# First tile projected block by block, meta tokens second, row scaling moved behind the input projection

## The chip, the cores and the metric

The kernel runs on one core of one Trainium2 chip. The metric is the device time of one execution in microseconds (us). The kernel before took 2399.41 us, the median of three runs (2391.92, 2399.41 and 2402.00).

## The reference, cut to what matters

One encoder block over 1024 tokens of width 1024, with 16 learned meta tokens put in front. What the change touches is its first step, the normed input projection, and the order of the token tiles in it:

```python
h = jnp.concatenate([meta, x], axis=1)            # 16 + 1024 rows
a = rms_norm(h, attn_norm_g[l])                   # x * rsqrt(mean(x*x) + eps) * g
proj = a @ w_in[l]                                # 1024 -> 1184 columns
q_s, k_s, v_s, q_lat, kv_lat, k_rope = jnp.split(proj, split_at, axis=-1)
# widths 512, 128, 128, 256, 128, 32
q_s, k_s = rms_norm(per head of 64, both)         # windowed attention
q = rms_norm(q_lat, g) @ w_q_up; kv = rms_norm(kv_lat, g) @ w_kv_up
q, k = rms_norm per head, then rope on 32 of 96   # latent attention
...
h = h + jnp.concatenate([y_a, y_b], axis=-1) @ w_out[l]
h = h + moe_ffn(rms_norm(h, ffn_norm_g[l]), ...)
return h[:, N_META:]                              # meta rows are dropped
```

The meta tokens serve as keys and values only; their queries are not needed for the output. Row scaling by the root of the mean square commutes with the product by `w_in`, which is what lets it be done behind the projection.

## The kernel before, in words

The program has three stages with a barrier between them: `project` (this change), `attend` and `experts`. Each is written by hand as one instruction stream for each engine, with semaphores between them; there is no scheduler. Every engine works strictly in the order in which its stream is written.

`project` goes over nine tiles of rows: eight real tiles of 128 and, as the last (t = 8, `MT`), the 16 meta tokens. SyncE (SP) loads tile 0, then the eight 128-row blocks of `w_in`, then the other tiles into three buffers `xt`. For one tile:

- `x_stats` (ScalarE) sums the squares and takes the root; `x_norm` (VectorE, L349) takes the reciprocal and multiplies the whole 128x1024 tile by it.
- `transpose_x` (TensorE, L488) turns the scaled tile into two PSUM banks; `norm_copy` on ScalarE (first four blocks) and on VectorE (last four) copies them to `normT`.
- `proj_part` (TensorE, L478) makes the 1184 columns in three parts of 512, 160 and 512, each over eight blocks of `w_in`, each in its own bank; `proj_copy` (ScalarE, L256) copies each part to `proj`. In the trace every fp32 matmul is two records, so a part is 16.
- The chain behind it, called the post work here: VectorE squares and sums `proj`, ScalarE takes roots, VectorE scales the heads (`qn`) and latents (`lat`) and signals `lat_ready`; TensorE transposes them (jobs `qpairs`, `lats`), makes the up projections (`kv0`, `kv1`, `q0`, `q1`); VectorE norms and rotates the heads (`k_ready`, `q_ready`); TensorE transposes them (`kT0` to `qT1`); ScalarE copies every job out of three rotating banks.

The main loop runs in steps s from -1 to 8. In step s TensorE does, in this order, part 0 of tile s+1, the transposes behind `lat_ready` of tile s, part 1 of tile s+1, the up projections of tile s, part 2 of tile s+1, the transposes of tile s+2, and the head transposes of tile s. So the projection of the next tile lies in the waits of the post work of this one. On VectorE a step begins with `x_norm(s + 2)`, which waits for ScalarE's `x_stats(s + 2)`, and only then comes the post work. `w_in` is multiplied by the norm's gain on VectorE (L369), block by block; TensorE waits for all eight blocks before its first projection:

```python
if s == -1:
    pe.wait_ge(w_scaled, DC)
proj_part(s + 1, 0)
```

After `project`, `attend` starts with its own loads: its first VectorE work waits for the load of `sink`, issued at the start of the stage.

Of the kernel before, what the change touches and what calls it, by code (L numbers as in the profile page):

```python
# [20 lines left out]
ALU = mybir.AluOpType  # L21
# [87 lines left out]
def project(nc, io, keep):  # L109

    with ExitStack() as ctx:
# [54 lines left out]
        x_normed = m.sem("x_normed")  # L166
# [21 lines left out]

        jobs = []
        for t in range(MT + 1):  # L190
# [25 lines left out]
        with nc.Block() as block:  # L216

            @block.sync
            def _(sp):
                def load_x(t):  # L220
                    if t >= 3:
                        sp.wait_ge(xT_done, 2 * (t - 2))
                    src = io["meta_tokens"] if t == MT else io["x"][0, t * P:(t + 1) * P, :]
                    sp.dma_start(xt[0:rows(t), t % 3, :], src).then_inc(x_in[t % 3], 16)
# [4 lines left out]
                for t in range(1, MT + 1):  # L229
                    load_x(t)  # L230

            @block.gpsimd
            def _(pool):
                nc.gpsimd.memset(mla_g[:], 1.0).then_inc(gains_one, 1)
                for t in range(MT + 1):
                    n = rows(t)
                    pool.wait_ge(proj_out, 3 * t + 3)
                    nc.gpsimd.tensor_copy(swa_v[0:n, t, :], proj[0:n, t % 2, C_V:C_QL]).then_inc(v_copied, 1)

            @block.scalar  # L240
            def _(act):
# [6 lines left out]
                def x_stats(t):  # L248
                    n = rows(t)
                    act.wait_ge(x_in[t % 3], 16 * (t // 3 + 1))  # L250
                    link(nc.scalar.activation(square[0:n, :], xt[0:n, t % 3, :], ACT.Square,
                                              accum_out=x_stat[0:n, t, 0:1]))
                    nc.scalar.activation(x_stat[0:n, t, 1:2], x_stat[0:n, t, 0:1], ACT.Sqrt,
                                         scale=1.0 / D, bias=keep["eps"][0:n, :]).then_inc(x_root, 1)

                def proj_copy(t, part):  # L256
# [38 lines left out]
                def norm_copy(t):  # L295
                    if t >= 2:
                        act.wait_ge(proj_done, 3 * (t - 1))
                    act.wait_ge(xT_done, 2 * t + 1)
                    nc.scalar.copy(normT[:, t % 2, 0:4, 0:rows(t)],
# [1557 lines left out]
```

## Time and profile before

| | |
|---|---|
| median of three runs | 2399.41 us |
| the profiled execution, its own time | 2405.51 us |
| its span, first to last instruction | 2403.9 us |
| TensorE busy | 2267.3 us (94%) |
| VectorE, ScalarE, GpSimd busy | 779.9, 459.1, 216.2 us |
| stage `project`, from the start to the first matmul of `attend` | 256.76 us |
| mean granted TensorE clock | 0.971 |

All durations below are of the one profiled execution, which was 6.1 us above the median of the other runs. In the rows of a timeline the columns are the start and the duration in us, the engine, line and operation, what is written and read, the shapes, the count, and in brackets the idle time before it on this engine with what ended it. PE is TensorE, PEld its weight loads, DVE VectorE, ACT ScalarE. A row with a count merges neighbours.

### The profile page before, as it was taken

How to read it: one execution, taken by the hardware profiler on the slowest of the kernel's cores; microseconds unless marked ns; L12 is line 12 of the kernel's file. 1: busy time of each engine (PE TensorE's matmuls, PEld its weight loads, DVE VectorE, ACT ScalarE, POOL GpSimd, SP SyncE). 2: the span in 40 equal slices, each digit the busy share in tenths (PEclk: the TensorE clock that was granted, in tenths of full speed). 3: DMA queues.
4: the chain of work that ended last, by engine and by line, in shares of the span. 5: the costliest groups of instructions: out<-in, count | busy, mean ns of one | idle time of the engine just before them, and what ended most of it. 6: DMA issues, size and time to landing. Idle time of an engine off the chain costs nothing.

```text
span 2403.9 us, 36883 instructions
## 1 busy us (share of the span) xinstructions
PE 2267.3 (94%) x15236; PEld 1702.6 (71%) x15236; DVE 779.9 (32%) x2243; ACT 459.1 (19%) x1148; POOL 216.2 (9%) x248
## 2 busy tenths in 40 slices
PE   6999799999999639999999999999999999999997
PEld 3554466666666437788877887788788787887875
DVE  3555344454444412222222222222222222222221
ACT  2333334453444300000001000100000000100000
POOL 0000000000000110111111111111010000100000
PEclk9999799999999859999999999999999999999999
DMA  4000500000000196778887988799989989899881
GB/s 153 27 2 1 160 10 28 18 10 28 27 27 28 38 345 226 251 250 291 282 308 250 308 312 317 264 312 321 339 309 339 343 311 339 307 336 346 307 304 19
DMA packets 212010, 492.26 MB, mean 205 GB/s; under 512 B 24608, under 2 KB 28480, under 8 KB 211664
## 3 DMA queue, kind: packets, MB, share of 16 engines
q1 hardware_dynamic: 183888, 449.53, 51.2%
q0 software_dynamic: 16080, 38.27, 7.0%
q10 hardware_dynamic: 11872, 2.06, 0.5%
q8 instruction: 123, 2.02, 0.3%
q14 instruction: 47, 0.39, 0.0%
HBM read 464.59 MB, written 29.82 MB: 206 GB/s over the span
## 4 chain that ended last, share of the span: by engine, by line
PE 63%; ACTq 1%; DMA 1%; DVE 0%; issue 0%; POOL 0%; ACT 0%; POOLq 0%; DVEq 0%
PE gu_bank L1676 40%; PE ya_bank L1690 18%; PE yb_bank L1703 3%; PE xa_bank L1646 1%; ACTq L1489 1%; DMA tri_e<-in_tri 1%; PE xb_bank L1654 0%; ACTq L1487 0%; ACTq L1492 0%; POOL out_y L1425 0%; ACT y_rows L1503 0%; DVE y_rows L1561 0%; PE yb_bank L1713 0%; DVE xT L1577 0%; PE yb_bank L1711 0%
## 5 line engine op out<-in xcount | busy, mean ns | idle before, releaser
L1676 PEld LDWEIGHTS gu_bank<-xT,ring 128*128 128x128 f32 x8192 | 964.6, 191 | 15.7 <-issue 15.7
L1676 PE MATMUL gu_bank<-xT,ring 128*128 128x128 f32 (+10 forms) x8192 | 968.1, 281 | 1.0 <-DVE xT L1577 1.0
L1690 PE MATMUL ya_bank<-ring,hidden 128*128 128x512 f32 x1024 | 446.2, 594 | 0.0
L1690 PEld LDWEIGHTS ya_bank<-ring,hidden 128*128 128x128 f32 x1024 | 192.0, 190 | 230.0 <-issue 225.5
L1538 DVE TENSOR_SCALAR g_in<-gu_bank,bias_cur 128x128 f32<-128x128 f32 (+10 forms) x256 | 92.0, 359 | 683.7 <-PE gu_bank L1676 683.7
L1497 ACT ACTIVATE sig<-g_in 128x128 f32<-128x128 f32 (+10 forms) x256 | 81.0, 317 | 879.2 <-DVE g_in L1538 879.2
L1561 DVE TENSOR_TENSOR y_rows<-ya_bank,b_row 128x512 f32<-128x512 f32 x64 | 41.2, 686 | 383.1 <-PE ya_bank L1690 383.1
L484 PE MATMUL proj_bank<-w_in_sb,normT 128*128 128x512 f32 (+3 forms) x432 | 149.0, 499 | 13.5 <-DVE w_in_sb L369 12.7
L1425 POOL DMA_INDIRECT out_y<-y_rows,tab x32 | 51.9, 1620 | 960.9 <-ACT y_rows L1503 960.9
L1037 PE MATMUL score_bank<-mla_kT,mla_qT 96*128 96x512 f32 x256 | 137.2, 663 | 0.0
L1503 ACT ACTIVATE y_rows<-y_rows,tab 128x512 f32<-128x512 f32 x64 | 42.7, 714 | 478.2 <-DVE y_rows L1561 478.2
L484 PEld LDWEIGHTS proj_bank<-w_in_sb,normT 128*128 128x128 f32 (+1 forms) x432 | 70.6, 181 | 81.6 <-issue 78.2
L943 DVE TENSOR_REDUCE real_max<-score_bank 128x1 f32<-128x1024 f32 x64 | 78.4, 1225 | 118.1 <-PE score_bank L1037 117.9
L1158 PE MATMUL score_bank<-w_out_sb,mixedT 128*128 128x512 f32 x256 | 112.0, 595 | 1.6 <-issue 1.6
L792 ACT COPY probsT<-act_bank 128x512 f32<-128x512 f32 (+2 forms) x96 | 52.0, 542 | 245.4 <-PE act_bank L1060 199.6
L1158 PEld LDWEIGHTS score_bank<-w_out_sb,mixedT 128*128 128x128 f32 x256 | 48.0, 190 | 60.4 <-issue 60.4
L1541 DVE TENSOR_SCALAR u_in<-gu_bank,bias_cur 128x128 f32<-128x128 f32 (+10 forms) x256 | 89.7, 350 | 0.0
L551 POOL DMA_INDIRECT slot_table<-pair,slot_i x32 | 31.4, 981 | 543.7 <-DVE slot_i L912 535.7
L1550 DVE SCALAR_TENSOR_TENSOR hidden<-u_in,g_sig 128x128 f32<-128x128 f32 (+10 forms) x256 | 76.8, 300 | 8.8
L1037 PEld LDWEIGHTS score_bank<-mla_kT,mla_qT 96*128 96x128 f32 x256 | 47.7, 204 | 44.5 <-issue 44.5
L1547 DVE TENSOR_TENSOR g_sig<-g_in,sig 128x128 f32<-128x128 f32 (+10 forms) x256 | 74.4, 291 | 0.0
L1079 PE MATMUL mla_bank<-probsT,mla_v 128*64 128x128 f32 x1024 | 71.8, 284 | 0.0
(243 smaller groups left out, 1732.4 us busy)
## 6 DMA issues: line engine op xcount, KB each, us to landing
ring<-in_w_gate SPq DMA_DIRECT2D x64, 2048.0 KB, 12.9
ring<-in_w_up SPq DMA_DIRECT2D x64, 2048.0 KB, 10.9
ring<-in_w_down SPq DMA_DIRECT2D x64, 2048.0 KB, 14.0
b_row<-in_b_down SPq DMA_DIRECT2D x32, 512.0 KB, 9.9
w_in_sb<-in_w_in SPq DMA_DIRECT2D x8, 592.0 KB, 9.0
xt<-in_x SPq DMA_DIRECT2D x8, 512.0 KB, 4.0
resid<-in_x SPq DMA_DIRECT2D x8, 512.0 KB, 4.3
out_y<-resid SPq DMA_DIRECT2D x8, 512.0 KB, 2.6
```

What stands on the lines that cost most here:

```text
L484: last = nc.tensor.matmul(proj_bank[0:n, part, 0:c1 - c0], normT[:, t % 2, k, 0:n], w_in[:, k, c0:c1], start=(k == 0), stop=(k == DC - 1))
L943: link(v.tensor_reduce(real_max[:, n % 2:n % 2 + 1], score_bank[:, j % 2, :], AX.X, ALU.max))
L1037: last = nc.tensor.matmul(bank[:, half * 512:(half + 1) * 512], mla_qT[:, i, cols(t)], mla_kT[:, i, half * 512:(half + 1) * 512], start=Tr ...
L1158: last = nc.tensor.matmul(score_bank[:, j % 2, half * 512:(half + 1) * 512], mixedT[:, k, :], w_out[:, k, half * 512:(half + 1) * 512], st ...
L1497: nc.scalar.activation(sig[:, f % 2, 0:width], g_in[:, f % 2, 0:width], ACT.Sigmoid, scale=ALPHA)\
L1538: v.tensor_scalar(g_in[:, f % 2, 0:width], gu_bank[:, f % 2, 0:width], bias_cur[:, f:f + 1], LIMIT, ALU.add, ALU.min).then_inc(g_ready, 1)
L1541: v.tensor_scalar(u_in[:, f % 2, 0:width], gu_bank[:, f % 2, 256:256 + width], bias_cur[:, FC + f:FC + f + 1], 1.0 + LIMIT, ALU.add, ALU.min)\
L1547: v.tensor_tensor(g_sig[:, s % 2, 0:width], g_in[:, s % 2, 0:width], sig[:, s % 2, 0:width], ALU.mult).then_inc(g_sig_ready, 1)
L1550: v.scalar_tensor_tensor(hidden[:, s, 0:width], u_in[:, s % 2, 0:width], 1.0 - LIMIT, g_sig[:, s % 2, 0:width], ALU.max, ALU.mult).then_in ...
L1676: last = nc.tensor.matmul(gu_bank[:, f % 2, i * 256:i * 256 + width], w[:, k, c * P:(c + 1) * P], xT[:, k, 0:width], start=(k == 0), stop= ...
L1690: last = nc.tensor.matmul(ya_bank[:, h, :], hidden[:, k, 0:P], w[:, k % 4, h * 512:(h + 1) * 512], start=(k == 0), stop=(k == FC - 1))
L1703: last = nc.tensor.matmul(yb_bank[j * q:(j + 1) * q, 0:c], hidden[:, k, P:P + q], w[:, k % 4, j * c:(j + 1) * c], start=(k == 0), stop=(k ...
```

## The change

Four things are changed, all in `project`.

1. The tile is transposed as it was loaded. `x_norm` becomes `x_scale`, the reciprocal alone, and the scale is applied by ScalarE when it copies the projection out of PSUM (`proj_copy`).
2. The first tile is projected by `first_proj`: block k of `w_in` is used for all three parts as soon as that block has been multiplied by the gain. The transposes of the second tile stand ahead of it in TensorE's stream.
3. The order of the tiles is 0, meta, 1, ..., 7. What was counted by tiles is now counted by steps, through `order`.
4. Of the meta tile only 160 + 256 = 416 columns are projected (`meta_parts`): no windowed queries, no query latent.

ScalarE's stream has `norm_copy(0)` ahead of `x_stats(0)` and of the loads of the constants.

```diff
+        order = [0, MT] + list(range(1, MT))
+        LAST = len(order) - 1
+        meta_parts = [None, (C_KVL, C_END), (C_K, C_QL)]
...
             @block.sync
-                def load_x(t):
-                    if t >= 3:
-                        sp.wait_ge(xT_done, 2 * (t - 2))
+                def load_x(s):
+                    t = order[s]
+                    if s >= 3:
+                        sp.wait_ge(xT_done, 2 * (s - 2))
+                        sp.wait_ge(x_root, s - 2)
...
             @block.scalar
+                def proj_copy(s, part):
+                    t = order[s]
+                    if part_cols(t, part) is None:
+                        return
                     n = rows(t)
-                    c0, c1 = PROJ[part]
-                    if part == 0 and t >= 2:
-                        act.wait_ge(lat_ready, t - 1)
-                        act.wait_ge(v_copied, t - 1)
-                    act.wait_ge(proj_done, 3 * t + part + 1)
-                    nc.scalar.copy(proj[0:n, t % 2, c0:c1], proj_bank[0:n, part, 0:c1 - c0]).then_inc(proj_out, 1)
+                    c0, c1 = part_cols(t, part)
+                    if s >= 2:
+                        act.wait_ge(lat_ready, s - 1)
+                        act.wait_ge(v_copied, s - 1)
+                    act.wait_ge(x_scaled, s + 1)
+                    act.wait_ge(proj_done, parts_to(t, part))
+                    nc.scalar.activation(proj[0:n, s % 2, c0:c1], proj_bank[0:n, part, 0:c1 - c0], ACT.Copy,
+                                         scale=x_stat[0:n, s, 2:3]).then_inc(proj_out, 1)
...
+                norm_copy(0)
                 x_stats(0)
...
-                norm_copy(0)
                 x_stats(1)
+                norm_copy(1)
...
             @block.vector
-                def x_norm(t):
-                    n = rows(t)
-                    dve.wait_ge(x_root, t + 1)
-                    link(v.reciprocal(x_stat[0:n, t, 2:3], x_stat[0:n, t, 1:2]))
-                    v.tensor_scalar(xt[0:n, t % 3, :], xt[0:n, t % 3, :], x_stat[0:n, t, 2:3], None,
-                                    ALU.mult).then_inc(x_normed, 1)
+                def x_scale(s):
+                    n = rows(order[s])
+                    dve.wait_ge(x_root, s + 1)
+                    v.reciprocal(x_stat[0:n, s, 2:3], x_stat[0:n, s, 1:2]).then_inc(x_scaled, 1)
...
-                x_norm(0)
-
+                norm_copy(0)
                 dve.wait_ge(g_attn_in, 16)
                 for k in range(DC):
...
-                    if k == 1:
-                        norm_copy(0)
+                    if k == 3:
+                        x_scale(0)
...
+                    if t < MT:
+                        link(v.tensor_tensor(proj_sq[0:n, :], pr, pr, ALU.mult))
...
+                    else:
+                        v.tensor_tensor(proj_sq[0:n, C_K:C_V], pr[:, C_K:C_V], pr[:, C_K:C_V], ALU.mult)
+                        link(v.tensor_tensor(proj_sq[0:n, C_KVL:C_END], pr[:, C_KVL:C_END], pr[:, C_KVL:C_END], ALU.mult))
...
             @block.tensor
+                def first_proj():
+                    for k in range(DC):
+                        pe.wait_ge(w_scaled, k + 1)
+                        for part, (c0, c1) in enumerate(PROJ):
+                            last = nc.tensor.matmul(proj_bank[:, part, 0:c1 - c0], normT[:, 0, k, :],
+                                                    w_in[:, k, c0:c1], start=(k == 0), stop=(k == DC - 1))
+                            if k == DC - 1:
+                                last.then_inc(proj_done, 1)
+
+                def transpose_x(s):
+                    n = rows(order[s])
+                    pe.wait_ge(x_in[s % 3], 16 * (s // 3 + 1))
...
                         if s == -1:
-                            pe.wait_ge(w_scaled, DC)
-                        proj_part(s + 1, 0)
+                            transpose_x(1)
+                            first_proj()
+                        else:
+                            proj_part(s + 1, 0)
```

The first place is the start of TensorE's stream. `xT_bank<-ident_sb,xt` are the transposes of a loaded tile, `proj_bank` the projection, `job_bank` the post work. Before:

```order
L496 MATMUL xT_bank<-ident_sb,xt 128x128 x8
L484 MATMUL proj_bank<-w_in_sb,normT 128x512 x8
L484 MATMUL proj_bank<-w_in_sb,normT 128x160 x8
L484 MATMUL proj_bank<-w_in_sb,normT 128x512 x8
L496 MATMUL xT_bank<-ident_sb,xt 128x128 x8
L484 MATMUL proj_bank<-w_in_sb,normT 128x512 x8
L475 MATMUL job_bank<-ident_sb,qn 128x128 x4
```

And now:

```order
L550 MATMUL xT_bank<-ident_sb,xt 128x128 x8
L550 MATMUL xT_bank<-ident_sb,xt 128x16 x8
L537 MATMUL proj_bank<-w_in_sb,normT 128x512
L537 MATMUL proj_bank<-w_in_sb,normT 128x160
L537 MATMUL proj_bank<-w_in_sb,normT 128x512 x2
...
L517 MATMUL job_bank<-ident_sb,qn 128x128 x4
L517 MATMUL job_bank<-ident_sb,lat 128x128 x4
L529 MATMUL proj_bank<-w_in_sb,normT 16x160 x8
L581 MATMUL job_bank<-w_kvup,latT 128x512 x2
L586 MATMUL job_bank<-w_qup,latT 128x384 x4
L529 MATMUL proj_bank<-w_in_sb,normT 16x256 x8
```

The transposes of the second tile (meta, 16 wide) moved ahead of the first projection, and between the first projection and the first transposes of the post work no projection stands any more, where eight matmuls of 512 columns stood.

The second place is the end of TensorE's stream in `project`, the last two steps (`k_raw` and `q_raw` are the heads to be transposed). Before:

```order
L475 MATMUL job_bank<-ident_sb,qn 128x128 x4
L475 MATMUL job_bank<-ident_sb,lat 128x128 x4
L484 MATMUL proj_bank<-w_in_sb,normT 16x160 x8
L524 MATMUL job_bank<-w_kvup,latT 128x512 x2
L529 MATMUL job_bank<-w_qup,latT 128x384 x4
L484 MATMUL proj_bank<-w_in_sb,normT 16x512 x8
L475 MATMUL job_bank<-ident_sb,k_raw 96x128 x8
L475 MATMUL job_bank<-ident_sb,q_raw 96x128 x8
L475 MATMUL job_bank<-ident_sb,lat 128x16 x2
L524 MATMUL job_bank<-w_kvup,latT 16x512 x2
L475 MATMUL job_bank<-ident_sb,k_raw 96x16 x8
```

And now:

```order
L529 MATMUL proj_bank<-w_in_sb,normT 128x512 x8
L517 MATMUL job_bank<-ident_sb,k_raw 96x128 x8
L517 MATMUL job_bank<-ident_sb,q_raw 96x128 x8
L517 MATMUL job_bank<-ident_sb,qn 128x128 x4
L517 MATMUL job_bank<-ident_sb,lat 128x128 x4
L581 MATMUL job_bank<-w_kvup,latT 128x512 x2
L586 MATMUL job_bank<-w_qup,latT 128x384 x4
L517 MATMUL job_bank<-ident_sb,k_raw 96x128 x8
L517 MATMUL job_bank<-ident_sb,q_raw 96x128 x8
```

The stage now ends with the whole post work of a real tile, with queries, where it ended with the short one of the meta tile.

The third place is the start of ScalarE's stream, now (before, `normT` stood behind the loads of the constants):

```order
L275 DMA ident_sb<-in_ident 128x128
L276 DMA g_attn<-in_attn_norm_g 128x8x1
L336 ACT_TABLE_LOAD
L336 COPY normT<-xT_bank 128x512
L282 ACTIVATE square,x_stat<-xt 128x1024
L284 ACT_TABLE_LOAD
L284 ACTIVATE x_stat<-x_stat,eps 128x1
L344 DMA g_ql<-in_mla_q_lat_norm_g 128x2x1
```

The copy of the first tile moved ahead of the constants' fifteen loads, which thereby moved behind it.

## Rows read from the trace of the kernel before

**Rows 1.** Timeline of the first 51 us: start, duration, instruction, idle before.

```profile
9.65 1.94 PE L496 MATMUL xT_bank<-ident_sb,xt 128*128 128x128 f32 x8 [9.65 <-DVE xt L353]
...
17.46 1.58 DVE L369 TENSOR_SCALAR w_in_sb<-w_in_sb,g_attn 128x1184 f32<-128x1184 f32 x2 [7.96 <-DMA g_attn<-in_attn_norm_g]
...
24.27 17.66 PE L484 MATMUL proj_bank<-w_in_sb,normT 128*128 128x512 f32 x48 [12.67 <-DVE w_in_sb L369]
...
41.96 0.59 ACT L263 COPY proj<-proj_bank 128x512 f32<-128x512 f32 x1 [6.57 <-PE proj_bank L484]
...
44.44 0.16 DVE L352 RECIPROCAL x_stat<-x_stat 128x1 f32<-128x1 f32 x1 [0.91 <-ACT x_stat L253]
...
45.31 1.38 DVE L408 TENSOR_TENSOR proj_sq<-proj 128x1184 f32<-128x1184 f32 x1
...
50.64 0.66 PE L475 MATMUL job_bank<-ident_sb,qn 128*128 128x128 f32 x4
```

**Rows 2.** DMA issues from 5.9 us, and at 142.8 us: size, us to landing.

```profile
w_in_sb<-in_w_in SPq DMA_DIRECT2D x1, 592.0 KB, 12.4
xt<-in_x SPq DMA_DIRECT2D x1, 512.0 KB, 13.7
...
xt<-in_meta_tokens SPq DMA_DIRECT2D x1, 64.0 KB, 2.0
```

**Rows 3.** Timeline of TensorE's weight loads in the first projection.

```profile
25.26 0.33 PEld L484 LDWEIGHTS proj_bank<-w_in_sb,normT 128*128 128x128 f32 x1 [0.52 <-issue]
26.11 0.33 PEld L484 LDWEIGHTS proj_bank<-w_in_sb,normT 128*128 128x128 f32 x1 [0.52 <-issue]
```

**Rows 4.** Timeline of one step in the middle, 195 to 218 us.

```profile
196.53 1.04 ACT L251 ACTIVATE square<-xt 16x1024 bf16<-16x1024 f32 x1
...
198.20 0.74 DVE L353 TENSOR_SCALAR xt<-xt,x_stat 16x1024 f32<-16x1024 f32 x1
198.87 1.37 DVE L408 TENSOR_TENSOR proj_sq<-proj 128x1184 f32<-128x1184 f32 x1
...
204.19 0.66 PE L475 MATMUL job_bank<-ident_sb,qn 128*128 128x128 f32 x4 [1.63 <-DVE lat L429]
...
204.89 0.69 ACT L271 ACTIVATE swa_qT<-job_bank,swa_g 128x512 f32<-128x512 f32 x1 [1.63 <-PE job_bank L475]
...
207.30 1.88 PE L524 MATMUL job_bank<-w_kvup,latT 128*128 128x512 f32 x4
...
209.02 2.74 PE L529 MATMUL job_bank<-w_qup,latT 128*128 128x384 f32 x8
...
217.52 0.42 DVE L457 TENSOR_TENSOR q_raw<-proj_sq,head_root 128x256 f32<-128x256 f32 x1
```

**Rows 5.** Timeline of TensorE: starts of steps 1 and 7, then the stage's end.

```profile
67.53 4.89 PE L484 MATMUL proj_bank<-w_in_sb,normT 128*128 128x512 f32 x11
...
221.04 7.04 PE L484 MATMUL proj_bank<-w_in_sb,normT 128*16 128x512 f32 x16
...
229.03 2.35 PE L484 MATMUL proj_bank<-w_in_sb,normT 128*16 128x160 f32 x16
...
243.69 1.04 PE L475 MATMUL job_bank<-ident_sb,q_raw 128*96 128x128 f32 x8
...
247.81 0.29 PE L475 MATMUL job_bank<-ident_sb,lat 16*128 16x16 f32 x2 [3.08 <-DVE lat L429]
...
248.44 2.89 PE L524 MATMUL job_bank<-w_kvup,latT 128*16 128x512 f32 x4 [0.34 <-ACT latT L277]
...
256.76 3.57 PE L1026 MATMUL swa_bank<-mla_kT,mla_qT 96*128 96x16 f32 x16 [0.55 <-PEq L216]
```

**Rows 6.** Windows of the stage's end: busy times, PEclk (granted clock), DMA share, GB/s.

```profile
249.00:250.00 1.00, 1.00 (x3) 0.15 (x1) 0.00 (x0) 0.34 (x2) 0.00 (x0) 0.59 0.00 0
...
266.00:268.00 2.00, 0.86 (x2) 0.00 (x0) 0.00 (x0) 0.00 (x0) 0.00 (x0) 0.94 0.39 158
```

**Rows 7.** Timeline of `attend`: the first instruction of VectorE.

```profile
271.01 0.29 DVE L880 COPY meta_s<-swa_bank 128x128 f32<-128x128 f32 x1 [15.68 <-DMA sink<-in_swa_sink]
```

More of the change, by code:

```diff
@@ L185, in project, with part_cols, parts_to, parts_free @@
         pool_own = m.sem("pool_own_p")
+        order = [0, MT] + list(range(1, MT))
+        step_of = {t: s for s, t in enumerate(order)}
+        LAST = len(order) - 1
+        meta_parts = [None, (C_KVL, C_END), (C_K, C_QL)]
+        def part_cols(t, part):
+            return (meta_parts if t == MT else PROJ)[part]
+        def parts_to(t, part):
+            done = 0
+            for u in order:
+                for p in range(3):
+                    done += part_cols(u, p) is not None
+                    if (u, p) == (t, part):
+                        return done
+        def parts_free(t, part):
+            for u in reversed(order[:step_of[t]]):
+                if part_cols(u, part) is not None:
+                    return parts_to(u, part)
+            return 0
+        def tiles_to(s):
+            return sum(t < MT for t in order[:s])
         jobs = []
-        for t in range(MT + 1):
+        for t in order:
             names = ("qpairs", "lats", "kv0", "kv1", "q0", "q1", "kT0", "kT1", "qT0", "qT1")
@@ L228, in _ @@
                     sp.dma_start(w_in[:, k, :], io["w_in"][0, k * P:(k + 1) * P, :]).then_inc(w_in_in[k], 16)
-                for t in range(1, MT + 1):
-                    load_x(t)
+                for s in range(1, LAST + 1):
+                    load_x(s)
             @block.gpsimd
@@ L234, in _ @@
                 nc.gpsimd.memset(mla_g[:], 1.0).then_inc(gains_one, 1)
-                for t in range(MT + 1):
+                for s, t in enumerate(order):
                     n = rows(t)
-                    pool.wait_ge(proj_out, 3 * t + 3)
-                    nc.gpsimd.tensor_copy(swa_v[0:n, t, :], proj[0:n, t % 2, C_V:C_QL]).then_inc(v_copied, 1)
+                    pool.wait_ge(proj_out, parts_to(t, 2))
+                    nc.gpsimd.tensor_copy(swa_v[0:n, t, :], proj[0:n, s % 2, C_V:C_QL]).then_inc(v_copied, 1)
             @block.scalar
@@ L293, in job, with norm_copy @@
                     last.then_inc(job_out, 1)
[L295 to L299, printed above, removed]
-                                   xT_bank[:, 0, :].rearrange("p (k q) -> p k q", q=P)[:, :, 0:rows(t)])\
+                def norm_copy(s):
+                    n = rows(order[s])
+                    if s >= 2:
+                        act.wait_ge(proj_done, parts_to(order[s - 2], 2))
+                    act.wait_ge(xT_done, 2 * s + 1)
+                    nc.scalar.copy(normT[:, s % 2, 0:4, 0:n],
+                                   xT_bank[:, 0, :].rearrange("p (k q) -> p k q", q=P)[:, :, 0:n])\
                         .then_inc(normT_lo, 1)
+                norm_copy(0)
                 x_stats(0)
@@ L309, in _ @@
                         act.dma_start(dst, src).then_inc(const_in, 16)
-                norm_copy(0)
                 x_stats(1)
-                for s in range(-1, MT + 1):
+                norm_copy(1)
+                for s in range(-1, LAST + 1):
                     if s >= 0:
-                        n = rows(s)
-                        if s + 2 <= MT:
+                        t, n = order[s], rows(order[s])
+                        if s + 2 <= LAST:
                             x_stats(s + 2)
@@ L501, in _ @@
                 transpose_x(0)
-                for s in range(-1, MT + 1):
-                    n = rows(max(s, 0))
-                    if s + 1 <= MT:
+                for s in range(-1, LAST + 1):
+                    t = order[max(s, 0)]
+                    n = rows(t)
+                    if s + 1 <= LAST:
                         pe.wait_ge(normT_lo, s + 2)
```

148 lines of the change are left out of this document (75 added, 73 removed).

## The prediction, as put on record before the run

> **What bounds the kernel now.** I read the timeline of the first 51 us first, then one step in the middle, then the end of the stage, then the windows for the clock. All edits lie in `project`, the first 256.76 us [rows 5]; behind it `attend` starts by itself: its first VectorE work waits for its own load of `sink`, 14.3 us after the first matmul of the stage (271.01 - 256.76) [rows 7, 5]. So what `project` ends earlier or later should pass to the end one to one, and nothing more.
>
> Within `project` TensorE is the bound, with three exceptions. (a) The start: it stands idle until 24.27, when VectorE has scaled the last block of `w_in`; VectorE could begin at 17.46 only, when the gain's load had landed [rows 1]. (b) 1.63 us in each middle step, in which TensorE waits for `lat_ready` [rows 4]. (c) The end: from 244.73 (243.69 + 1.04) to 256.76, 12.03 us, only the meta tile's post work is left [rows 5]. Between these, step 0 ends at 67.53, the six steps 1 to 6 take 25.6 us each (221.04 - 67.53, over 6), step 7 takes 23.7 (to 244.73) [rows 5].
>
> I build the new stage from those pieces, as a sum of times along TensorE.
>
> **Start.** Transposing without the scaling takes the first transposes from 9.65 to about 6, which buys nothing, since the weights are not there. The first block is scaled at 17.46 + 0.79 = 18.3 [rows 1]; nothing in the change moves the gain's load. But TensorE's stream now has the transposes of the meta tile ahead of `first_proj`, and the meta tile's load is issued by SP behind all eight blocks of `w_in`. The last block landed 12.4 us after an issue at about 5.4, at 17.8, and the tile behind it 13.7 us after 5.95, at 19.7 [rows 2]. The 64 KB of meta rows took 2.0 us alone [rows 2], and in the queue I put them an eighth of a tile's 1.9 us behind the last block: 18.1. So the words "as the weights land" hold only in part: all the weights have landed when TensorE starts. Eight 16-wide transposes, about 1.1 us on a slow clock, give a start at 19.3, bounded by 18.3 (no wait for meta) and 21.0 (meta lands as late as a whole tile did). Of the expected start I take 5.0 us gained.
>
> The Trainium skill ("DMA: Bandwidth & Descriptors", Queues, rings and completion order) says that each DMA engine consumes the descriptors of one ring in order, which speaks against the block-by-block start, as here; it also says that loads are not finished strictly in that order. By the first the start is 19.3, by the second it could be 18.3. The two rows of landings above are in order.
>
> `first_proj` is the same 48 passes in another order, so again 17.66 us [rows 1], 1.6 of them the price of the half clock: weight loads 0.85 us apart at the start [rows 3] where 16 passes take 7.04 later, 0.43 each [rows 5]. VectorE needs 0.79 us for a block and TensorE 2.0 or more, so it does not starve. End: 37.0.
>
> ScalarE's part-2 copy with a scale takes 0.69 instead of 0.59, read from its copy of `swa_qT` with the scale of a partition [rows 4, 1]; the other copies are as long but lie in waits. Then come `x_stats` and VectorE's reciprocal (44.44 - 41.96 = 2.48 before, with a `norm_copy` of 0.5 in it that is gone): squares start at 39.2, and `lat_ready` comes 5.3 us later (50.64 - 45.31) [rows 1], at 44.6. The constants' loads are issued some 2 us later on ScalarE, because `norm_copy(0)` and a later `x_stats(0)` stand ahead; VectorE's work on them should then end near 34, before 37: no cost, and 3 us of room.
>
> **Step 0 loses its cover.** Before, part 0 of the next tile filled the wait for `lat_ready`. Now TensorE is idle from 37.0 to 44.6, 7.6 us. It was slow after the idle time before 24.27 [rows 1, 3], and at the stage's end the granted clock fell to half (1.2 GHz) at about 249.4, 4.7 us after the last dense work [rows 6, 5]; so I expect the half clock at 44.6. Full clock came back after 3.3 us (1.6 us lost at half speed) the first time, and only at about 266.1, 9.4 us after work resumed at 256.76, the second [rows 1, 3, 5, 6]. At full clock the step would take: from `qn`'s transposes to the kv matmuls 3.1 (207.30 - 204.19; the meta part of 160 columns costs the same 2.35 as a real one), from there to `q_ready` 10.6 (217.94 - 207.30) [rows 4, 5], and about 1.0 for the eight q transposes: 14.7. VectorE sets this length; the 256 columns of the meta part (half of 7.04) fit inside. With the half clock for 3.3 us it is 16.8, for 9.4 us 19.9; I take a return after 5 us, 17.7. Step 0 ends at 62.3, before 67.53: 5.2 gained.
>
> **Meta step.** Post work of the meta tile beside the projection of tile 1. It is like step 7 before (23.7), without the q up projections (2.6), `qn`'s transposes (0.5), q head transposes (0.9), with narrower k transposes (0.4) and `lat` (0.3), and with a tile to transpose (0.9): 19.9. Its shorter VectorE chain is done when TensorE's part 0 ends, so there is no wait.
>
> **Middle steps.** Five with `x_scale` (s = 2 to 6), then s = 7. The 128x1024 multiply of 0.74 stood on the path to `lat_ready`: ScalarE's squares at 196.53, multiply at 198.20, squares of `proj` at 198.87, TensorE's wait of 1.63 [rows 4]. It goes, with 0.7 us a step, and a wait of 0.9 remains: 24.9 each, 124.5; I take 124.1, as the first follows a step without q copies. Step 7 is the old 23.7 (no `x_norm` there either) with transposes of a tile neither before nor now, the projection 128 wide instead of 16, which costs the same; less the small difference of banks, 23.3. Sum so far 62.3 + 19.9 + 124.1 + 23.3 = 229.6, where before step 7 ended at 244.73: 15.1 gained.
>
> **End.** Now a whole post work is bare. From the end of the q transposes: `lat_ready` 4.0 later (part 2 ended 2.1 earlier; copy and squares start 0.8 after that, then 5.3), 2.0 to the kv matmuls with no projection between, 10.6 to `q_ready` [rows 4], 1.9 for the last transposes and ScalarE's copies, 0.3 for the barrier: 18.9 against 12.03. TensorE idles 4 us, works 1.3, and later idles 9, so by the fall seen after 4.7 us of idle and light work [rows 5, 6] part of this runs at half clock: 0.4 at least (final transposes), 6.3 if all do (1.2 for the first transposes, 1.7 for kv, 2.6 for q, 0.8 for the last). I take 3.6: 22.5. `attend` starts at 252.1 instead of 256.8.
>
> **Sum.** Start -5.0; step 0 -0.2 more; meta step and middle steps against the old steps 1 to 7 -9.9 (167.3 for 177.2); end +10.5; in all -4.6. The profiled execution's 2405.5 would become 2400.9; it lies 6.1 above the median, so the prediction for the median is 2399.4 - 4.6 = 2395.
>
> **Rivals.**
> *The clock stays up.* Idle of 3.08 us at 247.81 left the clock full for a while [rows 5, 6], so both new gaps might cost little: step 0 14.7 and end 19.3, 6.2 less: 10.8 gained, 2388.6. Against it: the 12.67 us gap was followed by the half clock [rows 1, 3], and 7.6 is nearer to that than to 3.
> *The lost cover costs more than the start brings (slower).* If half clock holds through all of step 0, kv starts 7.2 after `lat_ready`, kv and q work is 4.3 longer, the last transposes 1 longer: 24.3, and 1.7 more is lost in the meta step's first matmuls, 8.3 above my figure; with the end all at half clock, 2.7 more. Then +6.4: 2405.8. It decides from a return of the clock later than 9.4 us after 44.6, the longest seen [rows 5, 6]. Against it: this work is busier than that at 256.76, for TensorE has no long wait in it.
> The Trainium skill ("TensorE: Matmul & The Clock Gate", HAM oscillation) holds that bursts of matmuls with waits between them can fall to the slow clock at each wait; by that both gaps are paid, which my sum does in part, and without it 2388.6 would stand. The trace agrees at 249.4.
> *The early start doesn't come.* Meta rows land with a whole tile's delay, start at 21.0: 1.7 less gained, 2396.5. *The wait (b) was not the multiply's.* If ScalarE's longer copies (0.1 each) or its order delay `x_stats` as much as the multiply took, 3.5 less: 2398.3.
>
> **How the numbers follow.** Forecast 0.60, clock stays up 0.14, slower rival 0.08, late start 0.08, no gain in (b) 0.05; 0.05 for something behind `project` that my reading leaves out. What this kernel's runs can tell from no change is about 0.5%, 12 us. The forecast and most rivals are within it. Faster by more needs the full clock and an early start, or the runs' own scatter of some 5 us on top: 0.16. Slower by more needs the slower rival and scatter: 0.06. Same 0.78. Range: from the clock rival with 18.3 and scatter, 2384, to near the slower rival, 2404.
>
> **What would show it.** Right: the first projection starts near 19.3, behind 16-wide transposes that waited for the meta load; TensorE waits about 7.6 us for `lat_ready` of tile 0, with PEclk 0.5 behind it; middle steps of 24.9 with waits of 0.9; the last q copies about 22 us after the last projection's step; `attend`'s first matmul near 252; everything behind shifted alone. Wrong: a start at 24 or later, steps of 25.6, the constants' work ending later than 37, or a difference that arises behind the first matmul of `attend`.

## The result and the profile after

The changed kernel took 2406.38 us (median of 8 runs, 2402.95 to 2409.61), the kernel before 2398.61 us (8 runs, 2391.92 to 2402.0): ratio 1.0036, 95% interval 1.0022 to 1.0049. So it is 0.36% slower, 7.8 us by the medians, where 4.6 us faster was forecast. The profiled execution took 2409.1 us (before 2405.51), its span is 2407.1 us (before 2403.9), 3.2 us more.

In the edited stage the forecast held in its parts, with 2.7 us gained where 4.6 were forecast; the loss arose 580 us behind it. Timeline of TensorE in the kernel after, in `project` (columns as in the timelines above):

```profile
19.62 1.00 PE L550 MATMUL xT_bank<-ident_sb,xt 16*128 16x16 f32 x8 [11.80 <-DMA xt<-in_meta_tokens]
20.55 19.23 PE L537 MATMUL proj_bank<-w_in_sb,normT 128*128 128x512 f32 x48
...
47.45 1.09 PE L517 MATMUL job_bank<-ident_sb,qn 128*128 128x128 f32 x4 [7.67 <-DVE lat L471]
...
64.04 7.03 PE L529 MATMUL proj_bank<-w_in_sb,normT 128*128 128x512 f32 x16
...
84.33 7.11 PE L529 MATMUL proj_bank<-w_in_sb,normT 128*128 128x512 f32 x16 [0.42 <-ACT normT L336]
...
116.03 0.66 PE L517 MATMUL job_bank<-ident_sb,qn 128*128 128x128 f32 x4 [0.89 <-DVE lat L471]
...
207.37 7.03 PE L529 MATMUL proj_bank<-w_in_sb,normT 128*128 128x512 f32 x16
...
229.33 1.26 PE L517 MATMUL job_bank<-ident_sb,q_raw 128*96 128x128 f32 x8
234.79 1.00 PE L517 MATMUL job_bank<-ident_sb,qn 128*128 128x128 f32 x4 [4.20 <-DVE lat L471]
...
237.38 3.78 PE L581 MATMUL job_bank<-w_kvup,latT 128*128 128x512 f32 x4 [0.74 <-ACT latT L313]
...
254.09 3.57 PE L1083 MATMUL swa_bank<-mla_kT,mla_qT 96*128 96x16 f32 x16 [1.03 <-PEq L245]
```

They are read against [rows 1, 4, 5]: the first projection waits for the meta tile's load, the wait for `lat_ready` in the middle steps is 0.89 for 1.63, the uncovered wait of step 0 is 7.67, and the stage ends with a bare post work, part of it at half clock (kv in 3.78 for 1.88). `attend` begins at 254.09, before 256.76: 2.7 us gained. On VectorE, in the same window, the last blocks of `w_in`:

```profile
20.99 3.06 DVE L405 TENSOR_SCALAR w_in_sb<-w_in_sb,g_attn 128x1184 f32<-128x1184 f32 x4
```

VectorE was done with the eighth block at 24.05. TensorE's 48 passes, begun at 20.55, stand in one row without a wait. So the waits for single blocks held nothing up, and they, in place of one wait for all eight, are what let the projection start 3.5 us before the last block was scaled.

| piece, us | before | forecast | after |
|---|---|---|---|
| first projection starts | 24.27 | 19.3 | 20.55 |
| it takes | 17.66 | 17.7 | 19.23 |
| `lat_ready` of tile 0, as TensorE goes on | 50.64 | 44.6 | 47.45 |
| step 0 from there to the next step | 16.9 | 17.7 | 16.6 |
| step 1 (before tile 1, now the meta tile) | 25.6 | 19.9 | 20.3 |
| steps 2 to 6 | 127.9 | 124.1 | 123.0 |
| step 7 | 23.7 | 23.3 | 23.2 |
| its end to `attend` | 12.0 | 22.5 | 23.5 |
| `attend` begins | 256.76 | 252.1 | 254.09 |
| `attend`, to ScalarE's first load of `experts` | 579.4 | 579.4 | 577.9 |
| from there to the first gate matmul | 49.6 | 49.6 | 58.2 |
| from there to the end | 1518.1 | 1518.1 | 1517.0 |

The span's 3.2 us are -2.7 - 1.5 + 8.6 - 1.1 (rounded). What TensorE waits for at the start of `experts` is the plan of the expert blocks on VectorE, which needs ScalarE's small loads; `tri_e` is the last of them. ScalarE's loads and VectorE's first plan instruction, before:

```profile
836.15 0.61 ACTq L1487 DMA_DIRECT2D biasT<-in_b_gate  x1
836.80 2.42 ACTq L1487 DMA_DIRECT2D biasT<-in_b_up  x1
839.26 20.39 ACTq L1489 DMA_DIRECT2D masks<-in_masks  x1
...
861.96 0.53 ACTq L1492 DMA_DIRECT2D tri_e<-in_tri  x1
...
877.64 0.18 DVE L1582 TENSOR_TENSOR picked_e<-placing,widths 32x32 f32<-32x32 f32 x1 [4.32 <-DMA tri_e<-in_tri]
```

And after:

```profile
831.97 0.61 ACTq L1544 DMA_DIRECT2D biasT<-in_b_gate  x1
832.61 4.80 ACTq L1544 DMA_DIRECT2D biasT<-in_b_up  x1
...
837.45 29.56 ACTq L1546 DMA_DIRECT2D masks<-in_masks  x1
...
869.38 1.52 ACTq L1549 DMA_DIRECT2D tri_e<-in_tri  x1
...
882.01 0.18 DVE L1639 TENSOR_TENSOR picked_e<-placing,widths 32x32 f32<-32x32 f32 x1 [2.42 <-DMA tri_e<-in_tri]
```

ScalarE is held in the issue of `masks` for 29.56 us instead of 20.39. The loads are the same; no line of this stage was changed. The difference begins with the first of them. DMA views of both from the start of the stage (size, us from issue to landing), before and then after:

```profile
biasT<-in_b_gate ACTq DMA_DIRECT2D x1, 128.0 KB, 7.1
biasT<-in_b_up ACTq DMA_DIRECT2D x1, 128.0 KB, 36.2
```

```profile
biasT<-in_b_gate ACTq DMA_DIRECT2D x1, 128.0 KB, 14.8
biasT<-in_b_up ACTq DMA_DIRECT2D x1, 128.0 KB, 46.7
```

The first bias load lands 7.7 us later after its issue. At the same time SyncE begins its 2 MB weight loads. Before, its first was issued 1.41 us behind ScalarE's first load, after, 0.98 us. SyncE's own instructions (view by source line, SyncE's address arithmetic and first load), before:

```profile
L1327 SPq FUSED_REGOPS  x1: 48/48/48, 837.0 to 837.0; - x1
L1327 SPq MOVE ring<-in_w_gate x1: 29/29/29, 837.5 to 837.5; - x1
L1327 SPq DMA_DIRECT2D ring<-in_w_gate x1: 426/426/426, 837.6 to 837.6; - x1
```

And after:

```profile
L1384 SPq FUSED_REGOPS  x1: 48/48/48, 832.8 to 832.8; - x1
L1384 SPq MOVE ring<-in_w_gate x1: 38/38/38, 832.9 to 832.9; - x1
L1384 SPq DMA_DIRECT2D ring<-in_w_gate x1: 420/420/420, 832.9 to 832.9; - x1
```

(Columns: count, ns min/median/max, first and last start.) Before, SyncE stood 0.4 us between two instructions (837.0 to 837.5, the first 48 ns long); after, it does not stand there. It stands elsewhere. SyncE's last load of `attend` and its first instruction of the barrier, before:

```profile
L765 SPq DMA_DIRECT2D ffn_rows<-normed_r x1: 319/319/319, 823.5 to 823.5; - x1
L734 SPq DRAIN  x1: 123/123/123, 823.9 to 823.9; - x1
```

And after:

```profile
L822 SPq DMA_DIRECT2D ffn_rows<-normed_r x1: 320/320/320, 819.3 to 819.3; - x1
L791 SPq DRAIN  x1: 107/107/107, 820.1 to 820.1; - x1
```

The load ends at 823.8 and the next instruction follows at 823.9 in the first; it ends at 819.6 and the next follows at 820.1 in the second. So the pause is now ahead of the barrier, where SyncE waits 12 us for the other engines anyway, and it costs nothing there. Counted through the traces of all 13 kernels, a pause of 0.44 to 0.45 us stands ahead of the 80th recorded instruction of SyncE in every one of them, six recorded waits more or fewer. The theory that was tested by the runs below: this pause belongs to a place in SyncE's instruction stream; the six added waits in `load_x` move it out of the start of `experts`, SyncE comes 0.43 us earlier against ScalarE, and ScalarE's small loads meet the weights before the first is done. The rival: the loss belongs to the edits of `project` or varies by itself.

The six waits stand in the change's diff, but among its four points they are not named. The tile is transposed as it was loaded, so its transposes no longer show that ScalarE has summed its squares, and a load into its buffer has to wait for both.

### The profile page after: what moved, and what is told of

The parts are those of the page before. It is cut to its first block, busy times and chain, and to the rows that moved or that the text cites. A ratio compares the mean times of both kernels' runs of the same rounds, so it can differ in the third digit from the quotient of the medians.

```text
span 2407.1 us, 36887 instructions
## 1 busy us (share of the span) xinstructions
PE 2262.8 (94%) x15220; PEld 1705.3 (71%) x15220; DVE 771.5 (32%) x2234; ACT 460.8 (19%) x1147; POOL 216.0 (9%) x248
## 4 chain that ended last, share of the span: by engine, by line
PE 63%; ACTq 2%; DMA 1%; DVE 0%; issue 0%; POOL 0%; ACT 0%; POOLq 0%; DVEq 0%
PE gu_bank L1733 40%; PE ya_bank L1747 18%; PE yb_bank L1760 3%; ACTq L1546 1%; PE xa_bank L1703 1%; DMA tri_e<-in_tri 1%; PE xb_bank L1711 0%; ACTq L1544 0%; ACTq L1549 0%; POOL out_y L1482 0%; ACT y_rows L1560 0%; DVE y_rows L1618 0%; PE yb_bank L1770 0%; DVE xT L1634 0%; PE yb_bank L1768 0%
## 5 line engine op out<-in xcount | busy, mean ns | idle before, releaser
L529 PE MATMUL proj_bank<-w_in_sb,normT 128*128 128x512 f32 (+3 forms) x368 | 121.7, 484 | 0.4 <-ACT normT L336 0.4
L529 PEld LDWEIGHTS proj_bank<-w_in_sb,normT 128*128 128x128 f32 (+1 forms) x368 | 60.5, 183 | 53.3 <-issue 48.6
```

What stands on the lines that cost most here:

```text
L529: last = nc.tensor.matmul(proj_bank[0:n, part, 0:c1 - c0], normT[:, s % 2, k, 0:n], w_in[:, k, c0:c1], start=(k == 0), stop=(k == DC - 1))
```

## The experiments

In all of them "before" is run beside them on the same chip; ratios are to it. The median of "before" itself was 2398.61 us in the first set of runs and 2402.56 to 2403.98 in the others, so times of different sets are compared by their ratios alone. "First load to gate" is the time from ScalarE's first load of `experts` to the first gate matmul.

| label | ratio (95%) | median us | `attend` begins | SyncE's first weight load after ScalarE's first load | first load to gate |
|---|---|---|---|---|---|
| before | | | 256.76 | 1.41 | 49.6 |
| after | 1.0036 (1.0022 to 1.0049) | 2406.38 | 254.09 | 0.98 | 58.2 |
| sp_waits_before | 1.0027 (1.0016 to 1.0038) | 2408.26 | 256.52 | 0.97 | 58.7 |
| sp_one_before | 1.0006 (0.9994 to 1.0019) | 2403.35 | 256.54 | 2.00 | 50.1 |
| sp_one_after | 0.9984 (0.9974 to 0.9994) | 2398.85 | 253.15 | 1.55 | 49.4 |
| sp_late_after | 0.9899 (0.9884 to 0.9913) | 2378.65 | 253.25 | 5.38 | 29.2 |
| hold_before | 0.9892 (0.9878 to 0.9907) | 2378.39 | 258.70 | 10.70 | 26.9 |
| hold_after | 0.9883 (0.9869 to 0.9897) | 2377.37 | 252.74 | 10.11 | 29.6 |
| hold_multiply | 0.9900 (0.9881 to 0.9920) | 2378.12 | 257.00 | 10.41 | 26.4 |
| hold_proj_first | 0.9895 (0.9875 to 0.9914) | 2375.72 | 252.40 | 10.64 | 27.6 |
| hold_fill | 0.9850 (0.9831 to 0.9868) | 2366.65 | 247.47 | 10.68 | 26.9 |
| hold_meta_last | 0.9836 (0.9817 to 0.9855) | 2364.34 | 244.11 | 10.74 | 27.4 |
| hold_last_fill | 0.9830 (0.9815 to 0.9846) | 2362.07 | 240.44 | 10.32 | 26.4 |

**The stream alone, `sp_waits_before`.** The kernel before, with

```diff
                     if t >= 3:
                         sp.wait_ge(xT_done, 2 * (t - 2))
+                        sp.wait_ge(x_root, t - 2)
```

> The kernel before with only the six additional, already satisfied waits for x_root on SyncE's stream in project, as the changed kernel has them. Theory A (SyncE's earlier start in experts, 0.43 us against ScalarE, comes from the other layout of its instruction stream): SyncE starts its first weight load about 1.0 us after ScalarE's first load, tri_e lands about 8 us later, and the kernel is 5 to 9 us slower than before: 2404 to 2408. Theory B (the lead comes from the timing of the stages or varies from run to run): 2396 to 2401, as before.

Theory A held: the lead fell to 0.97 us, the first bias load took 15.4 us, `attend` began as before (256.52), and the kernel was 0.27% slower, 6.5 us by the ratio (3.8 to 9.1). From ScalarE's first load to the gate matmul it took 9.1 us more than before; the changed kernel takes 8.6 us more. "Already satisfied" in the expectation was not so. What SyncE waited for up to 250 us:

```profile
SPq L225 <- PE xT_bank L497: 110.4, 6, 21.5
SPq L223 <- ACT x_stat L254: 24.4, 6, 10.7
```

(Columns: us in all, times, longest.) Each of the six waits for `x_stat` held SyncE for a while, but behind each it still waited for the transposes, so the new waits delayed no load: both kinds together are 134.8 us, and before the transposes alone were 134.1. `project` ended at the same time. Six waits that delay nothing cost what the change lost.

**The lead, `sp_one_after`, `sp_one_before`, `sp_late_after`.** One or eight superfluous loads of a register in front of SyncE's loop:

```diff
+                sp.value_load(keep["owner_i"][0:1, 0:1], min_val=0, max_val=E - 1)
                 for at in range(TURNS):
```

> The changed kernel with one superfluous register load (0.55 us with what follows it) ahead of SyncE's first weight load of experts, so that ScalarE's first small load leads it by about 1.6 us instead of 0.98. Theory (the lead decides, steeply: 0.97 and 0.98 us of lead gave 58.7 and 58.2 us from ScalarE's first load to the first gate matmul, 1.41 gave 49.6, 5.4 gave 29.2): 44 to 49 us, and a time 9 to 14 us below the changed kernel, 2392 to 2397 where the changed one takes 2406. Rival (not the lead but the layout itself, or some other thing that the waits changed, slows the small loads): 56 to 59 us, 2404 to 2408.

> The kernel before with the same one register load. Its lead should become about 1.5 to 2.0 us: 2.0 if the 0.41 us pause inside SyncE's first address arithmetic stays, 1.5 if the shifted stream moves it away. Theory: 42 to 48 us from ScalarE's first load to the first gate matmul instead of 49.6, the time 2 to 8 us lower than before. Rival (the lead is of no effect): 49.6 us and the same time.

> The changed kernel with eight superfluous register loads (about 0.3 to 0.4 us each, some 3 us in all) on SyncE ahead of its first weight load of experts. Theory (the lead of ScalarE's first small load over the first weight load decides: 1.41 us in the kernel before, 0.98 us in the changed one): with 4 us of lead the first bias load lands before the weights fill the engines, at 7 us or less instead of 14.8, and tri_e at least 8 us earlier: the kernel is 8 to 15 us faster than the changed one, 2391 to 2398. Rival (the lead does not matter): same time as the changed kernel, 2406.

The DMA view of sp_one_after in that place:

```profile
biasT<-in_b_gate ACTq DMA_DIRECT2D x1, 128.0 KB, 4.6
biasT<-in_b_up ACTq DMA_DIRECT2D x1, 128.0 KB, 36.1
```

With 1.55 us of lead the changed kernel went from 58.2 to 49.4 us and from slower to faster than before: ratio 0.9984, 3.8 us. I had expected 44 to 49 us and 9 to 14 us less than the changed kernel; by the ratios (0.9984 and 1.0036) it is 12.5 us less. The steep slope that I had put behind it was wrong. 0.97 and 0.98 us of lead gave 58 us, everything from 1.41 to 2.00 gave 49 to 50: a step, not a slope. 5.38 gave 29, and between 2.00 and 5.38 no run lies. So sp_one_before was a miss: I expected 42 to 48 us and 2 to 8 us less, and got 50.1 us and the same time. Its pause came three instructions earlier in the code, as three more stood ahead of it (0.45 us between two others), and was still in the way. sp_late_after was a miss in size: 8 to 15 us below the changed kernel expected, 33 by the ratios. What goes with the first step is the first bias load (14.8 and 15.4 us at 0.98 and 0.97 of lead; 7.1, 4.6 and 4.4 at 1.41, 1.55 and 2.00), though from 7.1 to 4.4 nothing more was gained. What goes with 29 us is the second one: it landed after 36 to 37 us at each lead from 1.41 to 2.00, and after 6.3 at 5.38. These runs put the step between 0.98 and 1.41 us; why it lies there, and what makes the pause itself, was not tried.

**Without the contention, `hold_before`, `hold_after`.**

```diff
+                sp.wait_ge(bias_in, 32)
+                sp.wait_ge(plan_in, 64)
                 for at in range(TURNS):
```

> The kernel before, with one edit in the stage experts: SyncE waits until ScalarE's seven small loads there (two biases, the four plan tables; not the masks) have landed before it issues its first weight load. My theory: the changed kernel wins about 4 us in the two stages ahead of experts (its start 831.97 against 836.15) and loses 8.5 us behind that point, because its small loads on ScalarE's queue land later while the 2 MB weight loads of SyncE run (the first matmul of TensorE comes 48.9 us after its barrier's end was passed at 834.5, against 43.7 before). Without that contention tri_e should land by about 852 instead of 877, and the kernel should be 10 to 20 us faster than before: 2380 to 2390. Rival (the small loads are slow by themselves, not by contention): tri_e lands as late as before, the weights come later, and the kernel is slower by up to 30 us.

> The changed kernel with the same one wait on SyncE. Theory: with the contention gone from both, only the gain of the first two stages is left, so this is 3 to 5 us faster than hold_before, where the changed kernel was 7.8 us slower than the kernel before. Rival (the loss arises elsewhere, in project or attend on runs other than the profiled one, or by a slower experts loop): this stays 5 to 8 us slower than hold_before.

Both are 1.1% faster than before: about 25 us for two waits, more than the 10 to 20 that I had expected of hold_before. DMA view of hold_after:

```profile
biasT<-in_b_gate ACTq DMA_DIRECT2D x1, 128.0 KB, 4.4
biasT<-in_b_up ACTq DMA_DIRECT2D x1, 128.0 KB, 6.3
masks<-in_masks ACTq DMA_DIRECT2D x1, 32.0 KB, 4.9
```

The second bias load takes 6.3 us instead of 36.2 and 46.7, so the small loads were slow by contention, not by themselves. The gate is now another, the gather of the token rows, in the timeline of hold_after:

```profile
856.99 1.97 PE L1705 MATMUL xa_bank<-ident_sb,x_rows 128*128 128x128 f32 x8 [12.23 <-DMA x_rows<-ffn_rows,tab]
```

In hold_before this wait is 7.51 us, and the first gate matmul waits another 2.81 us for its weights, which the hold has put off: the hold's own price begins there.

The change itself is then no longer slower (2377.37 against 2378.39). By the ratios it is 2.2 us faster, give or take 5, where the rival needed 5 to 8 us slower: that rules it out. My 3 to 5 us between the two are not resolved: the medians differ by 1.0 us, each ratio is known to 0.14%, 3.4 us. The profiles show 6.0 us in `attend`'s start (258.70, 252.74), of which `attend` itself took 4.5 back (574.2 and 578.6 us) and the way to the gate 2.7; `attend`'s length lay between 572 and 579 us in all profiles, of both orders.

**The pieces of `project`**, each on hold_after. The order of the tiles, `hold_meta_last`:

```diff
-        order = [0, MT] + list(range(1, MT))
+        order = list(range(MT + 1))
```

> hold_after with one edit: the tiles in the order 0 to 7, meta (as before the change), all else of the change kept (scale behind PSUM, first projection block by block, 416 columns for meta). Compared with hold_after (its attend began at 252.74). Theory: meta second costs the cover of step 0 (7.7 us idle of TensorE) and bares a whole post work at the end; with meta last the end is the meta tile's short one again (12 us instead of 23.5), while step 7 becomes shorter than 23.1 because only 416 columns stand in it. The first projection starts later, near 21.5, since the tile behind the weights is now 512 KB. attend begins at 243 to 246, and the kernel is 6 to 10 us faster than hold_after: 2367 to 2372. Rival (the order is what made the gain of 4 us in project): attend begins at 254 or later and the kernel is no faster than hold_after.

The theory held, with a little more gained than the 6 to 10 us expected. Its timeline:

```profile
21.42 17.38 PE L537 MATMUL proj_bank<-w_in_sb,normT 128*128 128x512 f32 x48
38.64 7.07 PE L529 MATMUL proj_bank<-w_in_sb,normT 128*128 128x512 f32 x16
46.38 0.66 PE L517 MATMUL job_bank<-ident_sb,qn 128*128 128x128 f32 x4 [0.67 <-DVE lat L471]
...
217.95 4.33 PE L529 MATMUL proj_bank<-w_in_sb,normT 128*16 128x160 f32 x16
...
244.11 3.57 PE L1083 MATMUL swa_bank<-mla_kT,mla_qT 96*128 96x16 f32 x16 [0.55 <-PEq L245]
```

Step 0 waits 0.67 us instead of 7.7, and `attend` begins 8.6 us earlier, although the first projection starts 1.6 us later than in hold_after, behind a whole tile's load. By the ratios it takes 11 us less than hold_after, give or take 6.

The clock, `hold_fill`: superfluous matmuls into a free PSUM bank, 7 before the wait for `lat_ready` in step 0, 4 before it in the last step, 5 before `k_ready` there.

```diff
+                        if s in (0, LAST):
+                            fill(7 if s == 0 else 4)
                         pe.wait_ge(lat_ready, s + 1)
```

> hold_after with 16 superfluous matmuls of 512 columns on TensorE where it would idle: 7 before the wait for lat_ready of step 0, 4 before that of the last step, 5 before the wait for k_ready of the last step. They write a PSUM bank that is free there. Theory: the half clock behind these waits costs 2 us in step 0 (16.6 us instead of 14.7) and about 4 us at the end (23.5 instead of 19); with TensorE kept busy, step 0 takes 15 us, the end 20 or less, attend begins at 247 to 250. Rival (the waits are those of VectorE's chain, and the clock behind them costs nothing, or the superfluous work runs over into the wait's end): attend begins at 252 to 255.

The theory held. Windows of the changed kernel behind the wait of step 0 and in the kv matmuls of the end (PEclk is the third column from the right):

```profile
48.00:50.00 2.00, 2.00 (x10) 1.41 (x9) 0.00 (x0) 1.26 (x3) 0.00 (x0) 0.50 0.00 0
...
238.00:240.00 2.00, 2.00 (x3) 0.67 (x2) 0.00 (x0) 0.51 (x2) 0.00 (x0) 0.50 0.00 0
```

The windows of hold_fill that answer to them:

```profile
48.00:50.00 2.00, 2.00 (x16) 1.30 (x14) 0.00 (x0) 0.54 (x3) 0.00 (x0) 1.00 0.04 8
...
236.00:238.00 2.00, 2.00 (x7) 1.12 (x6) 0.87 (x2) 1.15 (x4) 0.00 (x0) 1.00 0.00 0
```

At 2.4 GHz step 0 took 15.1 us from `qn`'s transposes to the next step (61.68 - 46.56) and the end 19.3 (247.47 - 228.22, the end of the last step's `q_raw`), as the row sums for the full clock said (14.7 and 18.9). In hold_after, with the half clock, they took 17.5 and 23.7. So the clock behind the two waits costs 2.3 and 4.5 us, 6.8 together. Of these 5.3 show in `attend`'s start (247.47 for 252.74), because the first projection of this execution took 19.19 us for 17.57. By the ratios it is 8 us of time, give or take 6.

The start, `hold_proj_first`: `first_proj()` ahead of `transpose_x(1)`.

> hold_after with first_proj ahead of the transposes of the meta tile in TensorE's stream, so that it waits for no load behind the weights. Theory: it starts at 18.7 (first block scaled) instead of 20.6; the transposes, 1 us, then stand behind it inside the idle time before lat_ready: attend begins 1.5 to 2 us earlier, 250.7 to 251.3, and the time is 1 to 2 us lower, which this measurement can hardly tell. Rival (a start in the slow clock ends at a fixed time, so that an earlier start buys half): 0.8 to 1 us.

It started at 18.48, 1.3 us before hold_after (19.79), and the projection took 18.06 instead of 17.57. `attend` began 0.3 us earlier. That is less than the 1.5 to 2 us expected and less than the rival's 0.8 to 1, and the gain in time is too small to tell. It was lost before `lat_ready` of tile 0, which came at 45.47, not before 45.01. ScalarE's timeline of hold_after shows why:

```profile
36.33 0.97 ACT L298 ACTIVATE proj<-proj_bank,x_stat 128x512 f32<-128x512 f32 x2 [15.58 <-PE proj_bank L537]
37.45 0.69 ACT L298 ACTIVATE proj<-proj_bank,x_stat 128x512 f32<-128x512 f32 x1 [0.15 <-PE proj_bank L537]
```

And that of hold_proj_first:

```profile
36.92 0.21 ACT L336 COPY normT<-xT_bank 128x64 f32<-128x64 f32 x1 [16.28 <-PE xT_bank L550]
37.03 1.55 ACT L298 ACTIVATE proj<-proj_bank,x_stat 128x512 f32<-128x512 f32 x3
```

In ScalarE's stream the copy of the meta tile's transposes stands ahead of the three copies of the projection. With the transposes behind the projection (which ended at 36.54, not 37.36), ScalarE waited for them until 36.92, and all three copies followed; in hold_after two of the three were done as the projection ended. For the early start to pay, that copy would have to move too; no run tried it.

VectorE's multiply, `hold_multiply`: a superfluous reduction of 560 columns behind `x_scale` from step 2 on.

> hold_after with a superfluous VectorE reduction of 560 columns (0.72 us by the rows of like width) behind each x_scale from step 2 on, where before the multiply of 0.75 us stood. Theory: the middle steps go back from 24.8 to 25.5 us, TensorE's wait for lat_ready from 0.89 to 1.6, attend begins 3.5 to 4.5 us later than in hold_after, 256 to 257. Rival (the steps got shorter by something else): attend begins at 253 to 254, steps of 24.8.

The wait came back, 1.64 us for 0.89, and `attend` began at 257.00, 4.3 us later (the times, 0.9900 and 0.9883 by the ratios, are not told apart):

```profile
116.89 0.66 PE L520 MATMUL job_bank<-ident_sb,qn 128*128 128x128 f32 x4 [1.64 <-DVE lat L474]
```

So a VectorE instruction of that length in that place is enough to give the 0.7 us a step back. Of the 4.3 us, 1.4 had come by `lat_ready` of tile 0 (46.43 for 45.01); half of that is the first of these reductions, which stands ahead of tile 0's post work, the rest a later start and a longer first projection.

**The best of both, `hold_last_fill`**: tiles 0 to 7 and meta, the hold, and eight superfluous matmuls in TensorE's waits of the last two steps.

> The two best versions joined: SyncE waits for the small loads, tiles in the order 0 to 7 and meta, and 8 superfluous matmuls in TensorE's waits of the last two steps. Theory: the half clock still costs hold_meta_last 2 us in the 160 columns of meta (4.33 us for 16 passes against 2.35) and about 2 us at the end and in attend's first matmuls: attend begins at 241 to 242.5 instead of 244.1; the time is 1 to 4 us below hold_meta_last, 2360 to 2363. Rival (VectorE's chain sets that end): 244 again.

`attend` began at 240.44. The time, 2362.07 us, is 1.70% below the kernel before (interval 1.54 to 1.85) and below the changed one; against hold_meta_last it is not told apart.

## Why the prediction was wrong

- **The sum for `project` was right** but for sizes: forecast 252.1, measured 254.09, with the gain and the costs where they were put. So 2.7 us were gained in it and not 4.6. Even that nearness is in part luck, since misses of both signs cancel: `lat_ready` of tile 0 came 2.9 us late, steps 0 to 7 took 1.9 us less than put, the end 1.0 more. The start came 1.2 us later than put (meta landed at 19.3, not 18.1), most of the way to the late-start rival's 21.0. The first projection took 1.6 us more, since the half clock lasted longer at its start in that execution: weight loads stood 0.85 us apart for 5.8 us, before for 2.7. In hold_after it took 17.57 and in hold_fill 19.19 with the same stream up to there, so this is no effect of the edit.
- **Two readings in the sum were off, with little effect.** The windows of [rows 6] (0.59 in 249 to 250, 0.94 in 266 to 268) put the fall of the clock at 249.2 and its return at 266.2, not 249.4 and 266.1. For step 0 the working adds some 0.5 us more than half of the slow time to 14.7 (17.7 for 5 us, where half of 5 gives 17.2), and no row shows that part. The half clock lasted 3.2 us there (47.45 to 50.64), not 5, and the step took 16.6.
- **The start block by block**: as forecast, TensorE waited for the meta rows behind all weights, and no wait for a single block held it after that. The meta load landed 13.4 us after its issue behind the weights, 2.0 alone [rows 2]. The Trainium skill ("DMA: Bandwidth & Descriptors", Queues, rings and completion order) says that each DMA engine takes the descriptors of one ring in their order; with that the trace agrees.
- **Step 0's lost cover and the bare end** were put at the right place and size, 7.6 us for 7.67 and 22.5 for 23.5; hold_meta_last shows that the order of the tiles gives away 8.6 us of `project`. Both waits were followed by the half clock, so the rival of the clock that stays up was not the case, and hold_fill puts its price at 6.8 us of the stage. The Trainium skill ("TensorE: Matmul & The Clock Gate", HAM oscillation) describes waits between bursts of matmuls after which the next burst starts at the slow clock; the trace agrees.
- **The removed multiply** was right: 0.7 us a step, shown by hold_multiply.
- **The step that failed** is the first paragraph's: "what `project` ends earlier or later should pass to the end one to one, and nothing more". `experts` begins with a race between ScalarE's small loads and SyncE's large ones, and TensorE waits for the small ones. The added waits on SyncE shifted its stream by six instructions, the pause of 0.45 us moved ahead of the barrier, and 0.43 us of ScalarE's lead went with it; that cost 8.6 us, three times the 2.7 us gained in `project`. sp_waits_before makes the loss without the change, sp_one_after has the change without the loss and is 3.8 us faster (interval 1.4 to 6.2), where 4.6 was forecast. The 0.05 for "something behind `project`" was the true case and had no price. The prediction's sum has no term for SyncE's six waits, neither for what they wait for nor for their place in the stream.
- **The slower rival** (half clock through all of step 0) was not what happened: full clock came back at 50.64, within step 0. That its 2405.8 lies near the measured 2406.38 is chance.

## What to carry to other kernels

A stage that starts with small loads on one queue and large ones on another is a race that the order of the code does not show; look at which small load the first instruction behind a barrier waits for, and let the large ones wait for it, which gave 25 us here for two lines. Before a change in one stage is judged by the whole time, compare the stages' starts; a change that adds or removes instructions can shift another stage's start, even where they delay nothing in their own. And work that covers a wait has two values, the wait itself and the clock behind it.

## What the runs showed of the hardware that I had not expected

- A load of 128 KB of bias took 4.4 us alone, and 15 us when 2 MB loads began on another queue 0.97 us later; the one behind it took 47 us for 6.3 alone.
- SyncE stood for 0.44 to 0.45 us once in each of the 13 traces, always ahead of its 80th recorded instruction: in the start of `experts` in before, hold_before and sp_one_before, and ahead of the barrier in the ten with the six more waits. What makes it no run shows.
- `attend`, unchanged, took from 572.4 to 579.4 us by the profiles. The granted clock was at half for 48 us of it in the shortest and for 64 us in the longest, in places that differ from run to run.
- The PEclk column of the windows reads 1.00 in the first projection (20 to 26 us in the kernel after) while the weight loads stand 0.85 us apart, twice the 0.43 later. There the spacing tells the clock, and the column does not.
